# Layer norm sums taken as columns per token, three low parts made by an adding DMA, and high products ahead of low ones

## The reference, cut to what matters

```python
def conformer_conv(x, w_in, b_in, conv_w, conv_b, ln_g, ln_b, w_out, b_out):
    a, g = jnp.split(x @ w_in + b_in, 2, axis=-1)
    h = a * jax.nn.sigmoid(g)
    h = lax.conv_general_dilated(h, ...) + conv_b      # 31 causal taps, depthwise
    h = jax.nn.silu(layer_norm(h, ln_g, ln_b))         # mean and variance over the 1024 features of a token
    return h @ w_out + b_out
```

## Time and profile before

| | us |
|---|---|
| median of 3 runs | 1458.6 (1458.36 to 1459.15) |
| the profiled execution, its own time | 1457.93 |
| its span | 1456.1 |
| granted TensorE clock | 1.00 |
| PE busy | 1442.8 (99%) |
| DVE busy | 929.2 (64%) |
| ACT busy | 631.2 (43%) |
| POOL busy | 210.9 (14%) |

### The profile page before, as it was taken

One profiled execution on the slowest core, in us unless ns is written; L12 is line 12 of the kernel. 1 busy time (PEld: TensorE's weight loads), 2 busy tenths in 40 slices (PEclk: granted clock), 3 DMA queues, 4 the chain that ended last, 5 costly groups with the idle time before them and its releaser, 6 DMA issues.

```text
span 1456.1 us, 19997 instructions
## 1 busy us (share of the span) xinstructions
PE 1442.8 (99%) x6852; PEld 1174.9 (81%) x6852; DVE 929.2 (64%) x1330; ACT 631.2 (43%) x999; POOL 210.9 (14%) x155
## 2 busy tenths in 40 slices
PE   9999999999999999999999999999999999999999
PEld 8788888888877898888888888766578888888887
DVE  7877773573645667767754756899998653544532
ACT  7444442342546665444432425777754322222210
POOL 4000000000302241000000004599611000000000
PEclk9999999999999999999999999999999999999999
DMA  5233233232422012332332333243313333232321
GB/s 191 86 101 101 88 103 113 78 104 81 131 81 69 30 60 87 101 102 87 101 116 72 102 96 92 87 130 88 102 33 105 111 102 99 90 104 95 102 94 50
DMA packets 42397, 137.01 MB, mean 94 GB/s; under 512 B 4960, under 2 KB 5984, under 8 KB 42336
## 3 DMA queue, kind: packets, MB, share of 16 engines
q1 hardware_dynamic: 41200, 133.80, 28.5%
q10 hardware_dynamic: 1136, 2.42, 0.4%
HBM read 129.85 MB, written 2.10 MB: 91 GB/s over the span
## 4 chain that ended last, share of the span: by engine, by line
PE 85%; POOL 7%; DVE 4%; ACT 2%; issue 1%; DMA 0%; ACTq 0%; POOLq 0%; DVEq 0%
PE bank L543 27%; PE bank L545 27%; PE bank L544 27%; POOL prod L532 6%; PE bank L691 1%; PE bank L719 1%; PE bank L704 1%; DVE bank L1622 1%; DMA cst<-cst_in 0%; DVE wlo L1273 0%; PE bank L584 0%; DVE hv L1746 0%; ACT res L1025 0%; DVE ylo L1712 0%; ACT whi L891 0%
## 5 line engine op out<-in xcount | busy, mean ns | idle before, releaser
L543 PE MATMUL bank<-xh,whi 128*128 128x512 f32 x1184 | 465.2, 393 | 1.5 <-DVE res L1561 0.7
L545 PE MATMUL bank<-xh,wlo 128*128 128x512 f32 x1184 | 461.2, 390 | 0.0
L544 PE MATMUL bank<-xl,whi 128*128 128x512 f32 x1184 | 461.0, 389 | 0.0
L891 ACT ACTIVATE whi<-raw 128x1024 fp32r<-128x1024 f32 x244 | 255.6, 1050 | 235.1 <-PE bank L545 233.8
L1273 DVE TENSOR_TENSOR wlo<-raw,whi 128x1024 fp32r<-128x1024 f32 x244 | 312.4, 1281 | 43.6 <-ACT whi L891 35.5
L543 PEld LDWEIGHTS bank<-xh,whi 128*128 128x128 f32 x1184 | 222.3, 188 | 55.8 <-issue 7.1
L544 PEld LDWEIGHTS bank<-xl,whi 128*128 128x128 f32 x1184 | 222.4, 188 | 46.7 <-issue 1.2
L545 PEld LDWEIGHTS bank<-xh,wlo 128*128 128x128 f32 x1184 | 222.3, 188 | 46.6
L543 PE MATMUL bank<-ahi,whi 128*128 128x512 f32 x608 | 236.7, 389 | 0.0
L544 PE MATMUL bank<-alo,whi 128*128 128x512 f32 x608 | 236.7, 389 | 0.0
L545 PE MATMUL bank<-ahi,wlo 128*128 128x512 f32 x608 | 236.6, 389 | 0.0
(11 more groups left out here) (183 smaller groups left out, 1315.6 us busy)
## 6 DMA issues: line engine op xcount, KB each, us to landing
raw<-w_ffn_up SPq DMA_DIRECT2D x88, 512.0 KB, 3.4
raw<-w_ffn_down SPq DMA_DIRECT2D x32, 512.0 KB, 3.4
raw<-w_mlp_up SPq DMA_DIRECT2D x32, 512.0 KB, 3.3
raw<-w_mlp_down SPq DMA_DIRECT2D x32, 512.0 KB, 3.3
raw<-w_ain SPq DMA_DIRECT2D x16, 512.0 KB, 3.3
raw<-w_ffn_down SPq DMA_DIRECT2D x16, 384.0 KB, 3.1
raw<-w_qkv SPq DMA_DIRECT2D x12, 512.0 KB, 3.4
raw<-w_wo SPq DMA_DIRECT2D x8, 512.0 KB, 3.5
```

What stands on the lines that cost most here:

```text
L543: nc.tensor.matmul(out_, hi, mh, start=first, stop=False)
L544: nc.tensor.matmul(out_, hi, ml, start=False, stop=False)
L545: return nc.tensor.matmul(out_, lo, mh, start=False, stop=last)
L891: nc.scalar.activation(whi[:, s, 0:tiles * P], raw[:, s, 0:tiles * P], ACT.Copy)\
```

## The change

The statistics take the data as the stationary operand: for each chunk, four blocks of 128 tokens of `hv` and four of its square are loaded as 128 x 128 and multiplied with two columns of ones, so that the sums come out with tokens on the partitions, in 16 columns of one bank (cleared once by a product with zeros). ACT's copy and the four turning products are gone, and DVE reads the sums from the bank. For the `aout` units 1, 2 and 3, ACT writes the negated high part into `wlo`, and POOL issues a DMA that adds the weights from DRAM to it, in place of DVE's three subtractions; SP's loads into these slots then wait for `hi_done`. In the layer norm's products, the two products with `yhi` are issued for all three units as soon as `yhi` is there, and the product with `ylo` after them. The fills change from 1, 6 and 11 to 7 and 9.

```diff
@@ -51,10 +51,11 @@
 PARTS = 9
 LAST_DIAGS = 5
 HC = 3
+ADDED = tuple(range(17, 20))
 SLOTS = 4
 AHEAD = 3
 WARM = 10
-LN_FILL = (1, 6, 11)
+LN_FILL = (7, 9)
 LN_UNITS = 3
 BAND_BANKS = (4, 5, 6, 7, 2, 3, 4, 5)
 KT = 8
@@ -242,6 +243,8 @@
         w_loaded = [sem(f"w_loaded{s}") for s in range(SLOTS)]
         hi_done = sem("hi_done")
         lo_done = sem("lo_done")
+        low_negated = sem("low_negated")
+        low_added = [sem(f"low_added{s}") for s in range(SLOTS)]
         chain_done = sem("chain_done")
         acc_free = sem("acc_free")
         setup = sem("setup")
@@ -303,7 +306,6 @@
         hv_ready = sem("hv_ready")
         hv_squared = sem("hv_squared")
         stats_done = sem("stats_done")
-        sums_out = sem("sums_out")
         moments = sem("moments")
         spread_ready = sem("spread_ready")
         spread_done = sem("spread_done")
@@ -343,7 +345,7 @@
             else:
                 eng.wait_ge(wo_free, j + 1 - wo_ends(j))
 
-        token_sums_of = tmp[:, 1, :]
+        no_sums = hc[:, 0, 0:4 * NBLK]
         scales_on_diagonal = tmp[:, 3, :]
         offsets_on_diagonal = gate[:, 0, :]
 
@@ -379,6 +381,31 @@
 
             return 2 * unit + 2 if isinstance(unit, int) and unit < 4 else unit + 5
 
+        def is_added(unit):
+
+            return isinstance(unit, int) and unit - ph["ain"].unit in ADDED
+
+        def low_parts(unit):
+
+            if isinstance(unit, int):
+                return unit + 1 - sum(ph["ain"].unit + e <= unit for e in ADDED)
+            return unit + 1
+
+        def added_in_slot(unit):
+
+            return sum(is_added(e) for e in range(unit % SLOTS, unit + 1, SLOTS))
+
+        def wait_low(eng, unit, passed=0):
+
+            if is_added(unit):
+                eng.wait_ge(low_added[unit % SLOTS], 16 * added_in_slot(unit))
+            else:
+                eng.wait_ge(lo_done, low_parts(unit) - (0 if isinstance(unit, int) else passed))
+
+        def passed(p):
+
+            return len(ADDED) if p.unit > ph["aout"].unit else 0
+
         def loads(base, i, k):
 
             return 16 * (i + (base + k) // SLOTS + 1)
@@ -394,14 +421,16 @@
                 if isinstance(unit, int) and unit < SLOTS:
                     free, at = None, unit - p.unit
                 elif isinstance(i, int):
-                    free, at = unit - SLOTS + 1, SLOTS * i + k
+                    free, at = low_parts(unit - SLOTS), SLOTS * i + k
                 else:
-                    free, at = sp.snap(unit - SLOTS + 1), sp.snap(SLOTS * i + k)
+                    free, at = sp.snap(unit - SLOTS + 1 - passed(p)), sp.snap(SLOTS * i + k)
                 if p.name == "ain":
                     at = at ^ 1
                 src = p.weights[at] if isinstance(at, int) else \
                     p.weights[bass.ds(at, 1)].rearrange("o p n -> p (o n)")
-                if free is not None:
+                if is_added(unit - SLOTS):
+                    sp.wait_ge(hi_done, unit - SLOTS + 1)
+                elif free is not None:
                     sp.wait_ge(lo_done, free)
                 sp.dma_start(raw[:, k, 0:p.tiles * P], src).then_inc(w_loaded[k], 16)
 
@@ -533,6 +562,10 @@
                         .then_inc(tapped_steps, 1)
                     adds += 1
                 made += POOL_TAPS[c]
+            for e in range(2 * C + 1, 2 * C + 1 + AHEAD):
+                pool.wait_ge(low_negated, ADDED.index(e) + 1)
+                nc.gpsimd.dma_start(wlo[:, e % SLOTS, :], ph["aout"].weights[e - 2 * C], accum_op=ALU.add)\
+                    .then_inc(low_added[e % SLOTS], 16)
             add_squares("mlp")
 
 
@@ -547,7 +580,7 @@
             def chain(p, i, k, hi, lo):
 
                 chain_no = p.chain + SLOTS * i + k
-                pe.wait_ge(lo_done, p.unit + SLOTS * i + k + 1)
+                wait_low(pe, p.unit + SLOTS * i + k, passed(p))
                 pe.wait_ge(acc_free, chain_no - 3)
                 for t in range(p.tiles):
                     w = slice(t * P, (t + 1) * P)
@@ -558,7 +591,7 @@
             def first_chains(name, norm_name, n=2):
 
                 p = ph[name]
-                pe.wait_ge(lo_done, p.unit + n)
+                wait_low(pe, p.unit + n - 1)
                 pe.wait_ge(acc_free, p.chain + n - 4)
                 for t in range(C):
                     if t == C - 2 and norm_name != "ffn0":
@@ -822,12 +855,16 @@
             def statistics(c):
                 if c == 0:
                     pe.wait_ge(rms_ready, RR["ain"] + 2)
+                    pe.wait_ge(hc_ready, 1)
+                    nc.tensor.matmul(norm[0][:, 0:4 * NBLK], ones[:], no_sums, start=True, stop=False)
                 pe.wait_ge(hv_ready, c + 1)
                 pe.wait_ge(hv_squared, c + 1)
-                nc.tensor.matmul(norm[0][0:GROUP, :], ones[:, 0:GROUP], hv[:, c, :],
-                                 start=(c == 0), stop=(c == C - 1))
-                nc.tensor.matmul(norm[0][GROUP:P, :], ones[:, 0:GROUP], sq[:, c % 2, :],
-                                 start=(c == 0), stop=(c == C - 1)).then_inc(stats_done, 1)
+                for at, x in ((0, hv[:, c, :]), (2 * NBLK, sq[:, c % 2, :])):
+                    for b in range(NBLK):
+                        mm = nc.tensor.matmul(norm[0][:, at + 2 * b:at + 2 * b + 2], x[:, b * P:(b + 1) * P],
+                                              ones[:, 0:2], start=False,
+                                              stop=(c == C - 1 and at > 0 and b == NBLK - 1))
+                mm.then_inc(stats_done, 1)
 
             for c in range(C):
                 if c == 0:
@@ -850,26 +887,24 @@
             p = ph["aout"]
             pe.wait_ge(acc_free, p.chain)
             fill(LN_FILL[0])
-            pe.wait_ge(sums_out, 1)
-            for b in range(NBLK):
-                mm = nc.tensor.matmul(norm[1][:, 2 * b:2 * b + 2], token_sums_of[:, b * P:(b + 1) * P],
-                                      cst[:, CST_ID:CST_ID + P:GROUP], start=True, stop=True)
-            mm.then_inc(sqsum_done, 1)
-            fill(LN_FILL[1])
             for j, spread in enumerate((scales_on_diagonal, offsets_on_diagonal)):
                 pe.wait_ge(spread_ready, j + 1)
                 for b in range(NBLK):
                     mm = nc.tensor.matmul(bank[6 + j][:, b * P:(b + 1) * P], ones[:], spread[:, b * P:(b + 1) * P],
                                           start=True, stop=True)
                 mm.then_inc(spread_done, 1)
-            fill(LN_FILL[2])
-            pe.wait_ge(lo_done, p.unit + LN_UNITS)
+            fill(LN_FILL[1])
+            for k in range(LN_UNITS):
+                wait_low(pe, p.unit + k)
             for t in range(C):
+                w = slice(t * P, (t + 1) * P)
+                pe.wait_ge(ln_hi, t + 1)
+                for k in range(LN_UNITS):
+                    nc.tensor.matmul(acc[k][:], whi[:, k, w], yhi[:, t, :], start=(t == 0), stop=False)
+                    nc.tensor.matmul(acc[k][:], wlo[:, k, w], yhi[:, t, :], start=False, stop=False)
                 pe.wait_ge(ln_lo, t + 1)
-                w = slice(t * P, (t + 1) * P)
                 for k in range(LN_UNITS):
-                    mm = three(acc[k][:], whi[:, k, w], wlo[:, k, w], yhi[:, t, :], ylo[:, t, :],
-                               t == 0, t == C - 1)
+                    mm = nc.tensor.matmul(acc[k][:], whi[:, k, w], ylo[:, t, :], start=False, stop=(t == C - 1))
                     if t == C - 1:
                         mm.then_inc(chain_done, 1)
             for k in range(LN_UNITS, p.units):
@@ -1192,6 +1227,13 @@
                                          bias=v("conv_b", c) if k == 0 else 0.0).then_inc(tapped_ready, 1)
 
             nc.scalar.activation(eps[:, 3:4], eps[:, 0:1], ACT.Sqrt)
+
+            def negate_high(e):
+
+                act.wait_ge(hi_done, p.unit + e + 1)
+                nc.scalar.activation(wlo[:, e % SLOTS, :], whi[:, e % SLOTS, :].bitcast(F32), ACT.Copy, scale=-1.0)\
+                    .then_inc(low_negated, 1)
+
             def square(c):
 
                 act.wait_ge(hv_ready, c + 1)
@@ -1241,11 +1283,11 @@
                     split_hi(p.unit, 0, 2 * c + AHEAD)
                     split_hi(p.unit, 0, 2 * c + 1 + AHEAD)
                     split_hi(p.unit, 0, 2 * c + 2 + AHEAD)
+                    for e in range(3):
+                        negate_high(2 * c + e + AHEAD)
             nc.scalar.activation(eps[:, 4:5], eps[:, 0:1], ACT.Sqrt)
             square(C - 2)
             square(C - 1)
-            act.wait_ge(stats_done, C)
-            nc.scalar.activation(token_sums_of, norm[0][:], ACT.Copy).then_inc(sums_out, 1)
             act.wait_ge(moments, 4)
             nc.scalar.activation(rms[:, 4 * NBLK:5 * NBLK], rms[:, 3 * NBLK:4 * NBLK], ACT.Sqrt).then_inc(rms_ready, 1)
             nc.scalar.activation(eps[:, 4:5], eps[:, 0:1], ACT.Silu)
@@ -1702,9 +1744,6 @@
                 if c:
                     collect(c - 1)
             collect(C - 1)
```

(7 more changed lines are left out.)

## The result

| | before | changed |
|---|---|---|
| median, us | 1458.66 (1458.36 to 1459.15, 6 runs) | 1465.65 (1464.65 to 1469.78, 6 runs) |
| profiled execution, us | 1457.93 | 1464.83 |
| span, us | 1456.1 | 1462.9 |
| granted clock, mean | 1.00 | 0.998 |

The medians differ by 7.0 us, where 3.3 us had been forecast and the range ended at 1465.0. The ratio, which is estimated from all the runs and is not the quotient of the two medians (1.0048), is 1.0054 (95% interval 1.0039 to 1.0068). The direction was right, the size was not, and the spread of the runs is new: 5.1 us between the fastest and the slowest, against 0.8 us before. The profiled execution is one of the three fastest.

What follows compares the result with a forecast made beforehand. PE, 99% busy, was taken as the bound: clearing (0.24 us) and serial statistics at 1.78 us a chunk put the moments 3.29 us later, at 1054.40, giving 1461.9 us beside the median; range 1458.6 to 1465.0 us.

Steps and rivals of the forecast that it cites:

- What bounds the stage, and that PE has no slack in it: Conv stage: PE never waits from 938 to 1035 us, so work added to it is late by its full length.
- The price of a chunk of statistics, 1.78 us: Statistics on PE: 16 records per chunk, 1.62 to 1.84 us, taken as 1.78 against 0.95 us before.
- The better row: Trace rows pricing a statistics record: four turning products at 0.115 us each gave 1.84 us; one hidden load gave 1.73 us.
- That these groups run at the clock of the rows they were priced from: Statistics of chunks 5, 6 and 7 behind convolve(7): no gap, 3 x 1.78 = 5.34 us, moments at 1054.40.
- The clock: Rival, chance 0.07: clock falls after 5 us of loads; slow fills and first spread cost 2.2 us, 1464.1 us or more.
- One of the signs that I had named for being wrong: In the profile after: fill records of more than 0.12 us would show the prediction wrong.
- DVE's stall of 2.1 us, covered by PE: Second eviction of chunk 7: DVE waits 2.1 us for PE, its later work slips, covered by PE's own delay.
- The low parts cost nothing: Low parts by ACT's negations and POOL's adding DMAs: cost nothing, with 0.2 us margin at the upper bound.
- upper bound of 8.1: Adding DMA: worst landing time of 8.1 us, taken from the plain loads of x at the head of the program.
- High products first is worth nothing: Layer norm's products: PE starts 0.7 us earlier, but its wait for wlo grows from 1.5 to about 2.2 us.
- hidden loads: Rival, chance 0.12: stationary loads of the statistics run under other work, giving 1457.1 to 1458.6 us.
- the fills at the head of the program: Row pricing the falling clock: 20 records in 4.61 us, 0.23 us each, as at 1.2 instead of 2.4 GHz.

Runs made afterwards that it cites:

- Experiment 6: Two kernels, wide_moved and then wide_fewer, which leaves out the products of the squares of chunks 0 to 4; 1461.84 us and 1457.57 us.
- experiment 4: Kernel before with the new statistics alone, each product taking 64 columns of ones and not two; 1463.61 us, +4.6 us, ratio 1.0032.
- experiments 1: Kernel before with the new statistics alone, two columns, low parts and order of products as before; 1466.62 us, +8.1 us, ratio 1.0062.
- experiment 7: Kernel before with only the low parts by the adding DMA, old statistics, products mixed as before; 1458.34 us, ratio 0.9999.
- experiment 2: Changed kernel with the old statistics, keeping low parts by the adding DMA and high products first; 1459.48 us, ratio 1.0007.
- wide64: Changed kernel with 64 columns of ones in each statistics product and a 512-column clearing product; 1464.61 us, +6.1 us, ratio 1.0037.
- stat5_ahead: Changed kernel with the statistics of chunk 5 ahead of convolve(7), leaving two groups behind it; 1467.66 us, +9.2 us, ratio 1.0058.
- rest_only: The kernel of experiment 2: changed kernel with the old statistics; 1459.48 us, ratio 1.0007.
- stats_only: The kernel of experiments 1: kernel before with the new two-column statistics alone; 1466.62 us, ratio 1.0062.
- rest_moved: rest_only with DVE's inverse of r1 moved from behind the layer norm to behind the last collect; 1457.16 us, ratio 0.9988.
- wide_moved: wide64 with DVE's inverse of r1 moved ahead as in rest_moved; 1461.84 us, +3.2 us, ratio 1.0021.
- wide_fewer: wide_moved without the products of the squares of chunks 0 to 4, so five groups have 8 records; 1457.57 us, 4.3 us less.
- stats_wide: The kernel of experiment 4: stats_only with 64 columns of ones in each statistics product; 1463.61 us, ratio 1.0032.

## Why the prediction was too low

- *What bounds the stage, and that PE has no slack in it:* right. Experiment 6 takes 4.46 us from the groups ahead of convolve(7) and gets 4.3 us back in the time.
- *The price of a chunk of statistics, 1.78 us:* too small. Chunk 4 started 4.18 us later (1038.25 against 1034.07); less the 0.24 us of clearing and the 0.19 us by which the stage began later in this profile, the four groups ahead of it grew by 3.75 us and not 3.32. Chunk 4 itself took 1.88 us, the groups behind it 1.83 us. That is 0.43 + 0.10 + 0.15 us; convolve(7) with the step to the next group took 9.59 and not 9.47 us. Together with the 0.19 us it is 0.99 us. The better row was the dearer one, L855, whose shape is the same: 1.84 us. Without the clock the moments would have come near 1055.4 us, 4.3 us late and not 3.3; experiment 4 measures 4.6 us for the whole, with 0.6 us of dearer clearing in it.
- *That these groups run at the clock of the rows they were priced from:* this is the step that failed. The sum took three groups "without a gap, 3 x 1.78". The last one ran at half the clock and cost 1.58 us more, so the moments came 5.86 us late. Behind it the fills ended 1.02 us after the first spread was ready, and DVE's first scaling came 0.95 us later still: 6.81 us in the profile, of which the clock is some 2.5. In medians experiments 1 and 4 give 3.5 us or more for the clock in a kernel with the new statistics alone. The clock stood among the rivals with 0.07 and 2.2 us, and with a wrong seat for the cost: I let the fall begin with the fills, where it began inside the statistics, and I charged the spreads, by when it was over. One of the signs that I had named for being wrong, fill records of more than 0.12 us, is what the profile shows (0.22 us).
- *DVE's stall of 2.1 us, covered by PE:* 2.35 us, and covered.
- *The low parts cost nothing:* right (experiment 7), with the landing at 7.8 us, near the upper bound of 8.1; but the three were issued within 2.8 us and ran side by side, not one behind another. ACT's negations ended at 1046.7, forecast 1046.6.
- *High products first is worth nothing:* right in the wait of 2.2 us. Whether it is quite nothing stays open: with this order more runs show 0.999 (eight of eleven in experiment 2, two of eleven in 7), and in two profiles (wide64, stat5_ahead) the clock fell behind the 2.2 us, in two (the changed kernel, rest_only) it did not.
- *Rivals:* hidden loads did not occur: a group of 16 records took 1.79 to 1.88 us at a clock of 1.00, 0.112 to 0.118 us a record. The row from which the rival of the clock took its price, the fills at the head of the program, lies in a stretch for which the profile gives a granted clock of 1.00 (0 to 10 us), though a record took 0.23 us there; the price of a fill came out all the same, 0.22 us at 0.50.

Open: why runs of one kernel differ so in their mean clock (some 6 to 18 us at half speed, by the estimate above), why the fall in stats_only came 1 us earlier, and why the clock can fall in the layer norm of a kernel with the old statistics (rest_moved) in one run and not in the next. No run tells that.

## What to carry to other kernels

A product whose moving operand has two columns costs a full load of the stationary operand, and several of them in a row are work at which PE looks busy in every view and can still lose its clock: price such a stretch at both levels of the clock, and give it more columns where they cost no time, as 64 did here. Before giving PE work to shorten the path of another engine, see whether PE has idle time before that work, not after it. An early start of products pays only when what is next in line (here the residual and `wlo`) comes earlier too; moving 3.3 us of DVE from behind the layer norm into a place that was already waiting did that, and the adding DMA had made the place.

## What the runs showed of the hardware that I had not expected

- Back-to-back float32 products of 128 x 128 with two columns: PE and PEld busy throughout, and the granted clock fell from 1.00 to 0.50 among them. With 64 columns, in the same time per record (0.113 us in wide_moved against 0.114 us in the changed kernel, behind convolve(7)), it stayed at 1.00 there in the profiles of wide64, wide_moved, wide_fewer and stats_wide.
- A wait of 2.2 us between dense products of 512 columns was followed by 0.50 in the profiles of wide64 (1087.1 to 1090.6) and stat5_ahead (behind 1092.1), and not in those of rest_only and the changed kernel.
- With the clock at 0.50 the load-bound records slow down as well: 0.21 to 0.22 us each in the last group and the fills of the changed kernel, against 0.11 to 0.12 us at 1.00.
- The adding DMA: 512 KB from DRAM onto SBUF, three issued by POOL in 2.8 us, 7.8 us to landing at the median. The plain loads of the same matrix by SP take 3.4 us at the median of eight, and 5.2 us at that of the three that ran beside the adding ones.
